# A two-block network on one core: one pair's refills in halves, two memory scores in a row, and value weights 32 bytes further

## The chip, the core and the metric

The kernel runs on one core of a Trainium2 chip. The metric is the device time of one execution in microseconds (us), the median of several. TensorE (PE) multiplies 128x128 stationary operands with streams of columns into PSUM, VectorE (DVE), ScalarE (ACT) and GpSimd (POOL) work between PSUM and SBUF, and SyncE (SP) issues the transfers from HBM. Each engine works through its own instructions in order and waits on semaphores.

## What is computed

A first block (a mixer with two convolutions, then a mixture of 32 experts, 2 of 8 in one of 4 groups for each token) and a second one of two layers (three kinds of attention, gates, attention over a memory, a feed-forward part), for 256 tokens of 1024 numbers, all in fp32. Cut to what the change touches:

```python
for e in range(N_EXPERTS):                       # first block, 32 experts
    act = jax.nn.silu(t @ w1[e]) * (t @ w3[e])
    out = out + combine[:, e:e + 1] * (act @ w2[e])

for l in range(2):                               # second block
    xn = rmsnorm_2(x, norm_mix[l])
    (qa, ka, va, qb, kb, vb, qc, kc, vc, ...) = jnp.split(xn @ w_in[l], offsets, axis=-1)
    ...
    o = rmsnorm_2(o, subln) * (1.0 - lambda_init)      # in diff_attention
    ...
    # memory_cross_attention: 4 heads of 64, 256 memory tokens
    sc = jnp.einsum('bqhd,bmhd->bhqm', q, kv[:, :, 0]) * HEAD_DIM ** -0.5
    p = jax.nn.softmax(sc, axis=-1)
    o = jnp.einsum('bhqm,bmhd->bqhd', p, kv[:, :, 1])
```

## The kernel before

**Experts.** The experts are taken in 16 pairs (PAIRS), the two of a pair side by side in 64 columns each. A pair reads w1, w3 and w2, each as two transfers of 2 MiB. They go to six slots of `ring` (w1 of even pairs to 0 and 1, w3 to 2 and 3, w2 to 4 and 5) and to two spare places in `wp` and `hs` (w1 of odd pairs). The pairs are numbered from 0; what is called the second pair here is pair 1. On PE `turn` does one pair: the w1 product and the w3 product (`expand`, L1343), the transposes of the hidden part (L1403), the way back to the tokens of the pair before (`scatter`, L1332), and the w2 product (`contract`, L1425); `gather` (L1305) brings the tokens of the next two pairs. The first two pairs stand apart from the loop over the others.

SP issues the refills in one order. `w1_done`, `w3_done` and `w2_done` tell it that a pair's product has been finished and the slots are free. For the first pair `half_done` tells it a quarter earlier each: `load_quarters` refills behind it in four parts. The w3 weights of pair 1's first expert lie elsewhere (`attic`), loaded early. From the second pair on a slot is refilled in whole transfers (`pair_after`, L815; `load`, L782). The last pair comes in halves (`last_halves`, L845).

**Layers.** The weights of a layer come in pieces of 2 MiB to `raw_a` and `raw_b`. Each piece is cut in chunks of 1024 columns a partition, and each chunk is split in a high part `w_hi` (ACT, L1748) and a low part `w_lo` (DVE, L662, some on POOL), in four buffers (PARTS) taken in turn. PE multiplies high by high, low by high and high by low. For all pieces but the values' the weights are the stationary operand and `h_parts` (or `act_parts`) the moving one, 256 columns: L1063, L1064 and L1071, and L1726 to L1729 for the last product. For the values (V_A, V_B, V_C) `h_parts` is stationary and the weights move, 512 columns: L1523 to L1525. `h_parts` is 16 floats longer than its content and read from 8 floats on (H_SHIFT), 32 bytes. In the program's layout `w_lo`, `w_hi` and `h_parts` start at multiples of 128 bytes in a partition, before and after the change alike; `moe_parts`, which holds both operands of `gather` and `scatter`, and `act_parts` start 32 bytes past one.

**Order in a layer.** The list WORK is the order by hand, and every engine takes its own part of each step. Around the memory: cross_k, cross_q 0 (queries of the first two heads, L1099 and L1104), sums, then units 24 to 27 (two heads and half of the tokens each). For a unit: scores (PE, L1579), exp (DVE scales, L2488, and reduces, L2499; ACT's exp, L1745), probs (DVE, L2505 and L2513), turn (PE transposes, L1590), apply (PE, L1611). cross_q 1 (L1063 to L1071) gives the queries of units 26 and 27; ACT copies them (L1748). cross_v (L1677) is the values of the memory.

**PSUM** is four parts of 1024 floats that the steps take in turn; a step enters one when its tenant before has left. Scores 25 take the part that the sums of the cross norm leave (DVE, L2401).

## Time and profile before

| | us |
|---|---|
| median of 3 runs | 1608.95 |
| lowest and highest | 1607.92, 1609.51 |
| the profiled execution | 1607.3 |
| its span, first to last instruction | 1605.2 |
| PE busy | 1563.0 |
| DVE busy | 880.4 |
| ACT busy | 647.6 |

The profile is of one execution. Its page gives totals and the span in 40 slices of 40.1 us; views of the trace give single instructions, the chain of work that ended last and the rates of stretches. PE's busy time counts overlapping matmuls to their modelled ends, so the distance between two starts says more than a duration. In a timeline the bracket at a row's end is the idle time before it and what ended it.

### The profile page before, as it was taken

How to read it: one execution, taken by the hardware profiler on the slowest of the kernel's cores; microseconds unless marked ns; L12 is line 12 of the kernel's file. 1: busy time of each engine (PE TensorE's matmuls, PEld its weight loads, DVE VectorE, ACT ScalarE, POOL GpSimd, SP SyncE). 2: the span in 40 equal slices, each digit the busy share in tenths (PEclk: the TensorE clock that was granted, in tenths of full speed). 3: DMA queues.
4: the chain of work that ended last, by engine and by line, in shares of the span. 5: the costliest groups of instructions: out<-in, count | busy, mean ns of one | idle time of the engine just before them, and what ended most of it. 6: DMA issues, size and time to landing. Idle time of an engine off the chain costs nothing.

```text
span 1605.2 us, 25930 instructions
## 1 busy us (share of the span) xinstructions
PE 1563.0 (97%) x11055; PEld 1261.9 (79%) x11055; DVE 880.4 (55%) x1302; ACT 647.6 (40%) x1024; POOL 58.0 (4%) x28
## 2 busy tenths in 40 slices
PE   9999999899889999999999999999999999999998
PEld 8886434334444359989899899999989999899998
DVE  6943212112121148677877676647576878576653
ACT  2034212202202135464654554435464674554443
POOL 0000000000000000033000000000006000000000
PEclk9999999999999999999999999999999999999999
DMA  9177999999999995646244456474653543465550
GB/s 351 52 314 302 383 420 427 429 428 427 430 427 428 427 403 206 197 143 200 106 158 158 151 169 206 158 266 158 197 187 121 175 158 132 127 211 180 166 210 27
DMA packets 130086, 393.86 MB, mean 245 GB/s; under 512 B 4672, under 2 KB 60352, under 8 KB 117952
## 3 DMA queue, kind: packets, MB, share of 16 engines
q1 hardware_dynamic: 129984, 392.39, 64.9%
q8 instruction: 78, 1.28, 0.3%
q14 instruction: 24, 0.20, 0.0%
HBM read 386.34 MB, written 1.05 MB: 241 GB/s over the span
## 4 chain that ended last, share of the span: by engine, by line
PE 82%; DVE 9%; DMA 7%; issue 1%; ACT 1%; SPq 0%; DVEq 0%; ACTq 0%
PE psum L1343 12%; PE psum L1063 11%; PE psum L1064 11%; PE psum L1071 11%; DMA ring<-w 6%; PE psum L1425 5%; DVE outs L2119 3%; PE psum L1728 2%; PE psum L1726 2%; PE psum L1729 2%; PE psum L1305 2%; PE psum L1579 2%; PE psum L1524 1%; PE psum L1525 1%; PE psum L1523 1%; PE psum L1023 1%
## 5 line engine op out<-in xcount | busy, mean ns | idle before, releaser
L1063 PE MATMUL psum<-h_parts,w_hi 128*128 128x256 f32 x1472 | 364.7, 286 | 1.2 <-DVE w_lo L662 1.2
L1064 PE MATMUL psum<-h_parts,w_lo 128*128 128x256 f32 x1472 | 355.1, 279 | 0.0
L662 DVE TENSOR_TENSOR w_lo<-raw_a,w_hi 128x1024 fp32r<-128x1024 f32 x186 | 225.1, 1222 | 113.1 <-ACT w_hi L1748 112.1
L1063 PEld LDWEIGHTS psum<-h_parts,w_hi 128*128 128x128 f32 x1472 | 276.1, 188 | 13.7 <-issue 10.6
L1064 PEld LDWEIGHTS psum<-h_parts,w_lo 128*128 128x128 f32 x1472 | 277.5, 189 | 0.2
L1748 ACT ACTIVATE w_hi<-raw_a 128x1024 fp32r<-128x1024 f32 x202 | 210.7, 1055 | 159.8 <-PE psum L1071 64.9
L1071 PE MATMUL psum<-h_parts,w_hi 128*128 128x256 f32 x1472 | 201.9, 279 | 0.0
L1343 PE MATMUL psum<-ring,outs 128*64 128x512 f32 x704 | 168.4, 626 | 20.5 <-DMA ring<-w 20.5
L1071 PEld LDWEIGHTS psum<-h_parts,w_hi 128*128 128x128 f32 x1472 | 184.6, 188 | 0.0
L1343 PEld LDWEIGHTS psum<-ring,outs 128*64 128x64 f32 x704 | 57.2, 144 | 124.4 <-issue 124.4
L662 DVE TENSOR_TENSOR w_lo<-raw_b,w_hi 128x1024 fp32r<-128x1024 f32 x92 | 111.4, 1221 | 53.0 <-ACT w_hi L1748 52.7
L1748 ACT ACTIVATE w_hi<-raw_b 128x1024 fp32r<-128x1024 f32 x100 | 104.8, 1055 | 87.1 <-PE psum L1071 52.9
L2321 DVE SCALAR_TENSOR_TENSOR qk<-psum,rtok,qk 128x512 f32<-128x512 f32 x16 | 18.1, 1134 | 215.7 <-PE psum L1343 215.7
L1425 PE MATMUL psum<-ring,qk 128*64 128x512 f32 x512 | 113.2, 594 | 0.0
L2314 DVE SCALAR_TENSOR_TENSOR moe_parts<-psum,rtok,moe_parts 128x512 fp32r<-128x512 f32 x34 | 24.0, 746 | 137.9 <-ACT moe_parts L1745 137.9
L1726 PE MATMUL psum<-act_parts,w_hi 128*128 128x256 f32 x328 | 91.6, 279 | 0.0
L1728 PE MATMUL psum<-act_parts,w_hi 128*128 128x256 f32 x328 | 91.6, 279 | 0.0
L1729 PE MATMUL psum<-act_parts,w_lo 128*128 128x256 f32 x328 | 91.6, 279 | 0.0
L1748 ACT ACTIVATE qk<-psum 128x512 f32<-128x512 f32 (+2 forms) x28 | 16.7, 598 | 183.6 <-PE psum L1403 160.9
L1425 PEld LDWEIGHTS psum<-ring,qk 128*64 128x64 f32 x512 | 36.9, 137 | 62.7 <-issue 62.6
L662 POOL TENSOR_TENSOR w_lo<-raw_a,w_hi 128x1024 fp32r<-128x1024 f32 x16 | 38.6, 2418 | 1175.1 <-ACT w_hi L1748 1175.1
L983 PE MATMUL psum<-hs,ring 128*128 128x256 f32 x320 | 69.5, 379 | 0.2 <-DMA ring<-w_in 0.2
(318 smaller groups left out, 2535.0 us busy)
## 6 DMA issues: line engine op xcount, KB each, us to landing
ring<-w SPq DMA_DIRECT2D x70, 2048.0 KB, 15.9
raw_a<-w_in SPq DMA_DIRECT2D x20, 2048.0 KB, 8.3
raw_a<-w_gu SPq DMA_DIRECT2D x32, 1024.0 KB, 7.7
raw_b<-w_in SPq DMA_DIRECT2D x10, 2048.0 KB, 8.9
wp<-w SPq DMA_DIRECT2D x8, 2048.0 KB, 17.9
hs<-w SPq DMA_DIRECT2D x8, 2048.0 KB, 22.2
raw_b<-w_gu SPq DMA_DIRECT2D x12, 1024.0 KB, 7.1
raw_a<-w_down SPq DMA_DIRECT2D x8, 1536.0 KB, 6.4
```

The costliest lines, as they stand in the source:

```text
L662: return eng.tensor_tensor(chunk_part(w_lo, n), chunk_raw(n), chunk_part(w_hi, n).bitcast(F32), ALU.subtract)
L983: last = mm(view(duo(name), 0, 4, SEQ)[:, o, :], w[:, k, o * P:(o + 1) * P], hT[:, k, :], start=(k == 0 and o % 2 == 0), stop=(k == KD - 1 ...
L1063: mm(to, hi[:, k, :], h_hi[:, k, :], start=(k == 0), stop=False)
L1064: mm(to, lo[:, k, :], h_hi[:, k, :], start=False, stop=False)
L1071: last = mm(to, hi[:, k, :], h_lo[:, k, :], start=False, stop=(k == KD - 1))
L1343: last = mm(psum[rows, d, bank * 512:bank * 512 + 512], duo_tokens[k // 4][:, k % 4, cols], weights, start=(k == 0), stop=(k == KD - 1), s ...
L1425: last = mm(psum[rows, 2, half * 512:half * 512 + 512], hidT[:, f, rows], view(ring[:, at + e, :], 0, 4, D)[:, f, half * 512:half * 512 + ...
L1726: mm(to, hi[:, o, :], act_hi[:, k, :], start=(k == 0 and o % 2 == 0), stop=False, skip_group_check=True)
L1728: mm(to, hi[:, o, :], act_lo[:, k, :], start=False, stop=False, skip_group_check=True)
L1729: last = mm(to, lo[:, o, :], act_hi[:, k, :], start=False, stop=(k == KF - 1), skip_group_check=True)
L1748: return nca.activation(out_ap, in_ap, ACT.Copy)
L2119: ins = v.scalar_tensor_tensor(dst[:, k, :], src[:, k, j:j + SEQ], tap, dst[:, k, :], ALU.mult, ALU.add)
```

## The change

Four edits. (1) The transfers behind the second pair (w1 of pair 3, w3 and w2 of pair 2) are issued in two halves, by the new `load_halves`: the first half waits for `half_done`, which PE now raises in the middle of each of the second pair's products too, the second half for the product's end. PE waits for the first halves by semaphores that are free by then, and pairs 2 and 3 move out of its loop to stand apart. (2) Scores 25 come before cross_q 1. (3) Each buffer of `w_lo` and `w_hi` is 8 floats longer, and a chunk starts at 0 or at 8 floats in it, so that values' chunks lie 32 bytes past a multiple of 64 and all others at one. (4) The constant `mean_sub` goes; the sums of the sub-norm use `mean_model`, and ACT's square root scales by D / (2 CH).

```diff
+HALVES_IN = 48
...
-for _name, _width in (("ident", P), ("mean_model", P), ("mean_mixb", P), ("mean_head", P), ("mean_sub", P),
+for _name, _width in (("ident", P), ("mean_model", P), ("mean_mixb", P), ("mean_head", P),
...
-           ("sums", "cross"), ("scores", 24), ("exp", 24), ("cross_q", 21, 1), ("scores", 25), ("exp", 25), ("probs", 24),
+           ("sums", "cross"), ("scores", 24), ("exp", 24), ("scores", 25), ("cross_q", 21, 1), ("exp", 25), ("probs", 24),
...
-        w_lo = sb("w_lo", [P, PARTS, KD * P], F32R)
-        w_hi = sb("w_hi", [P, PARTS, KD * P], F32R)
+        w_lo = sb("w_lo", [P, PARTS, KD * P + H_SHIFT], F32R)
+        w_hi = sb("w_hi", [P, PARTS, KD * P + H_SHIFT], F32R)
...
-            return view(parts[:, BUFFER[n], :], 0, *dims)
+            return view(parts[:, BUFFER[n], :], H_SHIFT if is_values(i) == (BUFFER[n] % 2 == 0) else 0, *dims)
...
+            def load_halves(src, q, places, k, turned, done, part_full, part_of):
+
+                sp.wait_ge(half_done, turned)
+                for e in range(2):
+                    ks = slice(0, k // 2)
+                    sp.dma_start(view(places[e], 0, k, PIECE // k)[:, ks, :], src[2 * q + e, :, ks, :]).then_inc(part_of, 16)
+                sp.wait_ge(done, 3)
+                for e in range(2):
+                    ks = slice(k // 2, k)
+                    sp.dma_start(view(places[e], 0, k, PIECE // k)[:, ks, :], src[2 * q + e, :, ks, :]).then_inc(part_full[e], 16)
...
                     load_quarters(2, w2_v, 1, 4, 4, w2_done, x_half)
+                    load_halves(w1_v, 3, spare, KD, MIX_HALVES + 10, w1_done, spare_full, win1_part[1])
+                    load_halves(w3_v, 2, ring_at[1], KD, MIX_HALVES + 11, w3_done, full_at[1], ident_in)
+                    load_halves(w2_v, 2, ring_at[2], 4, MIX_HALVES + 12, w2_done, full_at[2], consts_in)
                 else:
...
-                pair_after(0, 0)
+                    pair_after(0, 0)
...
-                    if signal and quarter < 3:
+                    if quarter in signal:
                         last.then_inc(half_done, 1)
...
-                signal, second = early_pair == 0, early_pair == 1
+                signal = {0: (0, 1, 2), 1: (1,)}.get(early_pair, ())
+                second, third, fourth = (early_pair == i for i in (1, 2, 3))
...
+                    if fourth:
+                        pe.wait_ge(win1_part[1], HALVES_IN)
...
+                    if third:
+                        pe.wait_ge(ident_in, HALVES_IN)
...
+                    if third:
+                        pe.wait_ge(consts_in, HALVES_IN)
...
-                for pair in range(2):
-                    turn(p * PAIRS + pair, p, p * (PAIRS // 2), p * (PAIRS - 1) + pair, pair, None, pair)
-                with pe.Fori(1, PAIRS // 2 - 2) as q:
+                for n in range(4):
+                    turn(p * PAIRS + n, p, p * (PAIRS // 2) + n // 2, p * (PAIRS - 1) + n, n % 2, None, n)
+                with pe.Fori(2, PAIRS // 2 - 2) as q:
...
-                                last = mm(duo("subln")[:, at:at + 2], sq[:, k, t * P:(t + 1) * P], c("mean_sub")[:, 0:2],
+                                last = mm(duo("subln")[:, at:at + 2], sq[:, k, t * P:(t + 1) * P], c("mean_model")[:, 0:2],
...
-                        f(sub_roots, duo("subln")[:, 0:16], ACT.Sqrt, bias=eps[:]).then_inc(std_ready, 1)
+                        f(sub_roots, duo("subln")[:, 0:16], ACT.Sqrt, bias=eps[:], scale=D / (2 * CH)).then_inc(std_ready, 1)
```

SP's queue behind the quarters of the first pair, before: the last quarter of w2, then the refills behind the second pair (w1 to wp and hs, w3 and w2 to the ring), then the loop.

```order
L807 DMA ring<-w2 128x1024 [waits w2_done]
L807 DMA ring<-w2 128x1024
L782 DMA wp<-w1 128x4096 [waits w1_done]
L782 DMA hs<-w1 128x4096
L782 DMA ring<-w3 128x4096 [waits w3_done]
L782 DMA ring<-w3 128x4096
L782 DMA ring<-w2 128x4096 [waits w2_done]
L782 DMA ring<-w2 128x4096
L836 UNCONDITIONAL_BRANCH
```

The same place after the change:

```order
L816 DMA wp<-w1 128x2048 [waits half_done]
L816 DMA hs<-w1 128x2048
L820 DMA wp<-w1 128x2048 [waits w1_done]
L820 DMA hs<-w1 128x2048
L816 DMA ring<-w3 128x2048 [waits half_done]
L816 DMA ring<-w3 128x2048
L820 DMA ring<-w3 128x2048 [waits w3_done]
L820 DMA ring<-w3 128x2048
L816 DMA ring<-w2 128x2048 [waits half_done]
L816 DMA ring<-w2 128x2048
L820 DMA ring<-w2 128x2048 [waits w2_done]
L820 DMA ring<-w2 128x2048
```

Six transfers of 4096 floats a partition became twelve of 2048, the first two of each four behind `half_done`.

PE at the memory scores of a layer, before: the sums of the cross norm (L1086), scores 24, cross_q 1 (16 products in turn by L1063 and L1064, then L1071), and scores 25, scores 26 and the half of 27 in one row of five; then turn 24 and cross_v 0.

```order
L1086 MATMUL psum<-consts,std 128x2 x2
L1579 MATMUL psum<-qk 128x256 x2
L1063 MATMUL psum<-h_parts,w_hi 128x256
L1064 MATMUL psum<-h_parts,w_lo 128x256
...
L1071 MATMUL psum<-h_parts,w_hi 128x256 x8
L1579 MATMUL psum<-qk 128x256 x5
L1590 MATMUL psum<-consts,wp 128x128 x4
L1677 MATMUL psum<-raw_a,memT 128x256 x8
```

After (line numbers are those of the changed file, 15 or 22 higher here):

```order
L1101 MATMUL psum<-consts,std 128x2 x2
L1601 MATMUL psum<-qk 128x256 x4
L1078 MATMUL psum<-h_parts,w_hi 128x256
L1079 MATMUL psum<-h_parts,w_lo 128x256
...
L1086 MATMUL psum<-h_parts,w_hi 128x256 x8
L1601 MATMUL psum<-qk 128x256 x3
L1612 MATMUL psum<-consts,wp 128x128 x4
L1699 MATMUL psum<-raw_a,memT 128x256 x8
```

The two products of scores 25 moved ahead of the 24 of cross_q 1; nothing else moved.

## Rows read from the trace of the kernel before

**Rows 1.** The page: engines, clock and DMA in 40 slices, costliest groups.

```profile
PE   9999999899889999999999999999999999999998
...
DMA  9177999999999995646244456474653543465550
GB/s 351 52 314 302 383 420 427 429 428 427 430 427 428 427 403 206 197 143 200 106 158 158 151 169 206 158 266 158 197 187 121 175 158 132 127 211 180 166 210 27
...
L1063 PE MATMUL psum<-h_parts,w_hi 128*128 128x256 f32 x1472 | 364.7, 286 | 1.2 <-DVE w_lo L662 1.2
...
L1726 PE MATMUL psum<-act_parts,w_hi 128*128 128x256 f32 x328 | 91.6, 279 | 0.0
```

**Rows 2.** The chain that ended last: start us, us, what.

```profile
192.12 6.92 PE psum L1425 x32
...
213.93 19.32 DMA ring<-w
233.39 8.76 PE psum L1343 x32
...
245.05 3.84 PE psum L1305 x32
...
468.34 8.80 PE psum L1343 x32
...
916.35 2.80 PE psum L1104 x24
```

**Rows 3.** Timeline of PE, the second pair and the fourth: start us, us, what.

```profile
170.89 0.59 PE L1343 MATMUL psum<-wp,outs 128*64 128x512 f32 x1
...
177.76 0.59 PE L1343 MATMUL psum<-vals,outs 128*64 128x512 f32 x1
...
233.39 8.74 PE L1343 MATMUL psum<-ring,outs 128*64 128x512 f32 x32 [3.44 <-DMA ring<-w]
```

**Rows 4.** Timeline of SP's queue (SPq) behind the second pair.

```profile
177.97 0.33 SPq L782 DMA_DIRECT2D wp<-w  x1
...
184.84 39.09 SPq L782 DMA_DIRECT2D ring<-w  x10
```

**Rows 5.** Stretches; the last three numbers are granted clock, DMA share, GB/s.

```profile
560.00:580.00 20.00, 19.92 (x110) 8.72 (x108) 4.99 (x5) 2.92 (x6) 0.00 (x0) 1.00 1.01 421
178.00:182.00 4.00, 4.00 (x20) 1.35 (x18) 0.00 (x0) 0.67 (x1) 0.00 (x0) 1.00 0.91 295
199.00:204.00 5.00, 5.00 (x26) 1.67 (x24) 1.41 (x2) 2.55 (x3) 0.00 (x0) 1.00 0.82 292
172.00:178.00 6.00, 6.00 (x30) 2.11 (x28) 1.24 (x2) 0.40 (x2) 0.00 (x0) 1.00 1.02 415
204.00:228.00 24.00, 23.92 (x128) 9.95 (x126) 5.67 (x7) 3.00 (x6) 0.00 (x0) 1.00 1.00 427
292.00:296.00 4.00, 3.86 (x10) 1.39 (x12) 0.00 (x0) 0.00 (x0) 0.00 (x0) 0.50 1.01 430
```

**Rows 6.** Timeline of the memory scores, first layer; the last row is the second's.

```profile
884.51 0.17 DVE L2401 RECIPROCAL rtok<-rtok 128x2 f32<-128x2 f32 x1 [2.94 <-ACT rtok L1745]
...
887.96 0.38 ACT L1748 ACTIVATE qk<-psum 128x256 f32<-128x256 f32 x1 [0.34 <-PE psum L1071]
...
888.60 0.75 DVE L2488 TENSOR_SCALAR wp<-psum,rtok 128x512 f32<-128x512 f32 x1 [2.12 <-PE psum L1579]
...
890.18 0.69 DVE L2513 TENSOR_TENSOR wp<-wp,stat 128x512 f32<-128x512 f32 x1
...
890.93 0.66 PE L1590 MATMUL psum<-consts,wp 128*128 128x128 f32 x4 [1.34 <-DVE wp L2513]
...
1388.85 0.66 PE L1590 MATMUL psum<-consts,wp 128*128 128x128 f32 x4 [1.34 <-DVE wp L2513]
```

**Rows 7.** Timeline of PE, a values' piece, its first and last product.

```profile
655.42 0.39 PE L1523 MATMUL psum<-w_hi,h_parts 128*128 128x512 f32 x1
...
666.39 0.40 PE L1525 MATMUL psum<-w_hi,h_parts 128*128 128x512 f32 x1
```

More of the change, by code:

```diff
@@ L1353, in expand_all, with first_weights @@
                     last = expand(places, duo_tokens, pair, d, bank, (2 * quarter, 2 * quarter + 1))
-                    if signal and quarter < 3:
+                    if quarter in signal:
                         last.then_inc(half_done, 1)
                 last.then_inc(done, 1)
-            def first_weights(duos, duo_tokens, pair, d, bank, signal=False, second_half=None):
+            def first_weights(duos, duo_tokens, pair, d, bank, signal=(), second_half=None):
                 for e in range(2):
@@ L1437, in turn @@
                             last = contract(half, [f])
-                        if signal and f < 3:
+                        if f in signal:
                             last.then_inc(half_done, 1)
```

## The prediction

> **What bounds the kernel now.** I read the page's slices first [rows 1]. From about slice 4 (140 us) to slice 14 (600 us) the DMA engines run at 9 tenths and 383 to 430 GB/s: that is the expert stage, which streams 16 pairs of experts through the ring. After it PE is busy at 9 tenths to the end while DMA idles half the time: the two layers are bound by PE. Then I read the chain that ended last through the expert stage [rows 2]. Every two pairs ((468.34 - 233.39) / 4 = 58.7 us) it passes from PE to a transfer into the ring (19.32 us in the row shown) and back; the last such piece ends where the row at 468.34 us begins, and from there to the end of the stage the chain is PE's and, for a microsecond each, DVE's: the weights are there before they are needed. So in the expert stage a microsecond counts if it is taken from the DMA engines before 468 us, and in the layers if it is taken from PE. PE's own pace hides nothing more than 3.44 us at the first of these waits (the row at 233.39 us, [rows 3]): that is the ceiling on what earlier transfers can give there.
>
> **Part 1, the second pair's slots in two parts.** Before, the six transfers of 2 MiB that follow the quarters (w1 of pair 3, w3 and w2 of pair 2) are issued when the second pair has finished each product: at 177.97 and 184.84 us [rows 4], and behind the w2 product at 192.12 + 6.92 = 199.04 us [rows 2]. Did the engines stand idle for that? In a stretch with a backlog they move 427 GB/s [rows 5]. From 178 to 182 us it is 295: (427 - 295) x 4 / 427 = 1.24 us lost. From 199 to 204 us it is 292: (427 - 292) x 5 / 427 = 1.58 us lost. At 184.84 us little can be lost, because w1 (9.8 us from 178) is still in flight. Together 2.8 us.
>
> Now the first halves go out half a product earlier. The second pair's w1 product runs from 170.89 to 177.76 us [rows 3] and its w3 product to 184.8 us [rows 4], so the first halves may start at about 174.3 and 181.2 us; w2's product runs from 192.12 to 199.04 us [rows 2], its half is over at 195.6 us. At 174.3 us the quarters still move at 415 GB/s, and do so to 178 [rows 5], so 1 MiB x 2 (4.9 us) joins a queue that isn't empty, and the second halves at 178 join it too. Backlog then: 8.4 MB from 178 us ends at 178 + 19.6 = 197.6 us at the earliest, after 195.6: the second hole closes as well. The next issue, w1 of pair 4, comes at 206 us, and w2 lasts until 197.6 + 9.8 = 207.4: at most a few tenths open there.
>
> The price: a half's pieces are smaller. Quarters move 415 GB/s, the halves at the end of the stage (560 to 580 us) 421, whole transfers 427 [rows 5]. 12.6 MB in halves cost 12.6 / 0.421 - 12.6 / 0.427 = 0.4 us. Net: 2.8 - 0.4 = **2.4 us**, with ends 1.0 (only the first hole closes, less the price) and 3.4 (the ceiling). It passes to the end: transfers that come 2.4 us earlier still meet a backlog at every later issue (the pair of transfers that PE waits for at 233.39 us was issued at 213 us and takes 9.8 us by itself, so 9 to 10 us of work stood before it), and slots come free earlier by the same. The waits that PE gets are for first halves, which land before the second ones it waits for in any case; SP waits on half_done with only the second halves behind it, whose own condition comes later. What I can't tell from before: the clock. After each of those waits PE runs some microseconds at the 1.2 GHz level (granted 0.50 from 292 to 296 us, [rows 5]), and the 32 matmuls behind the wait take 8.76 and 8.80 us where 32 of w2's product take 6.92 [rows 2]. Only the last of these (468.34 us) is on the path, and it stays; all at the lower level it would be 13.8 us, so it can move by -1.9 to +5, and I count nothing.
>
> The Trainium skill says something against this part: "SBUF — State Buffer", The DMA setup-cost knee, gives each transfer a roughly fixed 2 us that doesn't scale with bytes and asks for the largest single transfer. By it, six more transfers would cost, as an estimate, 12 us. In this trace the quarters show the fixed time hidden by the queue: it isn't paid in throughput while others are in flight.
>
> **Part 2, the order of the memory scores.** Before, cross_q 1 (24 matmuls, until 887.9 us, when ACT copies it) stands between scores 24 and scores 25 [rows 6]. DVE then scales scores 25 at 888.60, reduces them, and only then makes probs 24 (890.18), for which PE waits 1.34 us (turn 24 at 890.93; the same 1.34 in the second layer at 1388.85) [rows 6]. Now scores 25 run at about 884.85 (their PSUM part is free: DVE's L2401, which frees it, is at 884.51 [rows 6]). DVE scales and reduces them from 886.5 to 888.0, since it idles 2.12 us there; probs 24 follows, and turn 24 could start at 888.9. What is late next: the five products of scores 25, 26 and half of 27 run from 887.9 to 890.93 - 1.34 = 889.59, 0.33 us each. So cross_q 1 ends 0.65 us later, at 888.55; ACT's copy of it takes 0.38; scores 26 can't start before that, at 889.0, and with the half of 27 end at 889.97. Turn 24 starts there: 890.93 - 889.97 = **0.95 us** a layer. DVE and ACT behind it move by 0.9 to 1.1 us as well, so the next turns don't wait longer. Two layers: **1.8 us**, ends 1.0 and 2.1.
>
> **Part 3, values' weight parts 32 bytes off.** No instruction is added; 288 matmuls of 512 columns read w at another place (L1523 to L1525, 96 each), with h as the stationary operand. They follow each other every (666.39 - 655.42) / 47 = 233.4 ns [rows 7], twice the 2.80 / 24 = 116.7 ns of a product of 256 columns [rows 2]. Where do the operands lie? h_parts is read 32 bytes past a multiple of 64, w at a multiple: they differ, for values as for all others. In one place both lie 32 past: gather (L1305), all in moe_parts. There a product takes 3.84 / 32 = 120.0 ns [rows 2]: 3.3 ns more at the same size. After the change values' w lies where h does. If the same place costs 3.3 ns for each load of 128 weight columns, 288 x 3.3 = +1.0 us; if it goes with streamed columns, 6.7 ns and +1.9 us; if the row of L1305 has another reason, 0. A gain can't be excluded either, since 512 columns at 2.4 GHz are 213 ns: at most 288 x 20 = 5.8 us. I take **+1.0 us**, by the only row with both operands alike.
>
> The skill speaks of this too: "TensorE: Matmul & The Clock Gate", Step-by-step, gives PE two independent read ports, one for the moving and one for the stationary operand. By it the places don't matter and the term is 0. The row of L1305 against the others doesn't agree with that, unless its 3.3 ns come from something else.
>
> The smaller edits (mean_sub replaced by mean_model with a scale in ACT's sqrt, 64 KB less of constants) change no count and no size on the path: 0.
>
> **The sum.** -2.4 - 1.8 + 1.0 = -3.2 us. The profiled execution took 1607.3 us (span 1605.2), so it becomes 1604.1; it is 1.65 us under the median of 1608.95, so against the median **1605.7 us**.
>
> **Rivals.**
> - A, as above, 1605.7: chance 0.38.
> - B, the values' places don't matter: 1604.7. For it: one row alone speaks for a cost. 0.30.
> - C, the new place serves values better than the old one, by 1 to 5.8 us: 1599 to 1603.7. For it: 233 ns are 9% above the clock's 213. Against it: all other products, with operands placed as values' are now not, have the same 9%. 0.12.
> - D, one of the two gains doesn't come: the hole at 199 us stays, or a shorter wait at 230 us only becomes a longer or colder one at 468 us, or turn 24 finds another late partner: 1606.5 to 1608.5. 0.12.
> - E, slower, by one mechanism: with rows of 1032 floats, the parts of all other pieces move too. Buffers 1 and 2 then start 64 bytes off a multiple of 128, 0 and 3 don't; before, all four were multiples of 128. If PE's reads care about 128 bytes and not 64, half of 1472 x 3 + 328 x 3 = 5400 matmuls (each line three times, [rows 1]) change by up to 3.3 ns: 2700 x 3.3 = 8.9 us, 1614.6 us. It decides from some 1900 matmuls on. Against it: nothing in the trace has such a place, so nothing for it either. 0.08.
>
> A measurement of this kernel can tell 0.2%, 3.2 us, from no change; so A lies exactly on the line, half of it on each side. Faster: 0.19 + 0.22 + 0.12 = 0.53; slower 0.08; the same 0.39. The range that leaves out C's lower part and E: 1602.5 to 1608.5.
>
> **What the profile after would show.** The rate from 178 to 182 and from 199 to 204 us at over 400 GB/s, and the wait at 233.39 us shortened from 3.44 to about 1 us, ending at 231; the last DMA piece of the chain ending near 466. Turn 24 at its wait for DVE gone and 0.4 us for ACT's copy before scores 26. Values' matmuls every 236.7 ns (A), 233.4 (B), less (C). L1063 and L1726 unchanged at 116.7 ns, else E. I'd be wrong in part 1 if the holes close and the piece at 468 us doesn't move.

## The result, and the profile after

| | before | after |
|---|---|---|
| median of 6 runs, us | 1608.68 | 1615.0 |
| lowest and highest, us | 1607.4, 1610.74 | 1611.81, 1616.06 |
| the profiled execution's span, us | 1605.2 | 1614.0 |

The changed kernel is slower: 1.0031 times the time before, with a 95% interval of 1.0021 to 1.0042, some 5 us (3.4 to 6.8; the medians above differ by 6.3). Forecast were 1605.7 us and a range of 1602.5 to 1608.5; the time lies 6.5 us above the range, where rival E of the prediction stood (1614.6 us, chance 0.08).

Names below: "the other pieces" are all weight pieces but the values'. Their w is the stationary operand (L1078, L1079, L1086, L1748 to L1751 in the changed file; L1063, L1064, L1071, L1726 to L1729 before). "Place" is an address in a partition, modulo 128 bytes where nothing else is said, as it stands in the program's layout.

The page after, in the columns of [rows 1]; its first row is the busy time of the engines, which was PE 1563.0 before.

```profile
PE 1573.5 (97%) x11055; PEld 1276.5 (79%) x11055; DVE 880.6 (55%) x1302; ACT 647.5 (40%) x1024; POOL 57.9 (4%) x28
...
GB/s 348 50 313 272 403 428 427 428 429 428 428 429 427 428 389 197 193 157 184 109 153 157 158 186 179 168 253 161 212 174 122 169 154 132 130 209 188 152 209 27
...
L1078 PE MATMUL psum<-h_parts,w_hi 128*128 128x256 f32 x1472 | 367.8, 287 | 0.0
...
L1748 PE MATMUL psum<-act_parts,w_hi 128*128 128x256 f32 x328 | 92.2, 281 | 0.0
```

The same 11055 products keep PE busy for 10.5 us more. L1078 has 367.8 us where L1063 had 364.7, L1748 92.2 where L1726 had 91.6 [rows 1]. These lines were not rewritten: only where their weights lie changed. In the GB/s row the fifth and sixth slices stand at 403 and 428, for 383 and 420 before: the holes are gone.

The chain that ended last, after, in the columns of [rows 2]:

```profile
174.43 13.75 PE psum L1358 x64
...
216.88 17.17 DMA ring<-w
234.18 7.10 PE psum L1358 x32
...
469.26 8.80 PE psum L1358 x32
...
541.56 17.01 DMA ring<-w
558.71 7.10 PE psum L1358 x32
...
1107.32 2.86 PE psum L1119 x24
```

The second pair's products begin at 174.43 us, not at 171.07, so this execution was 3.36 us late before the change could act. From there to the row at 469.26, where the last refill that [rows 2] has too lets PE go on, it is 294.83 us. Before it was 468.34 [rows 2] less 171.07, from this row of the same view of the kernel before:

```profile
171.07 13.75 PE psum L1343 x64
```

That is 297.27 us, so 2.4 us are gained. The row at 541.56 us is a further piece on DMA that [rows 2] doesn't have; PE waited 0.34 us for it. The last row of the chain after is a group of 24 products: 2.86 us where [rows 2] has 2.80.

Stretches after, in the columns of [rows 5]: the two of the prediction, and the same two 3.4 us later, where this execution has the same work.

```profile
178.00:182.00 4.00, 4.00 (x22) 1.37 (x20) 0.00 (x0) 0.66 (x1) 0.00 (x0) 1.00 1.04 421
199.00:204.00 5.00, 5.00 (x26) 1.71 (x24) 0.83 (x2) 1.54 (x3) 0.00 (x0) 1.00 1.03 424
181.40:185.40 4.00, 4.00 (x20) 1.35 (x18) 0.00 (x0) 0.63 (x1) 0.00 (x0) 1.00 1.03 430
202.40:207.40 5.00, 5.00 (x27) 1.67 (x24) 1.41 (x2) 2.55 (x3) 0.00 (x0) 1.00 1.02 424
```

Both holes are closed, 430 and 424 GB/s for 295 and 292. Timeline of PE after, at the first wait of the expert stage, at the next one, and at the memory scores (columns as in [rows 3]):

```profile
234.18 7.09 PE L1358 MATMUL psum<-ring,outs 128*64 128x512 f32 x32 [0.85 <-DMA ring<-w]
```

```profile
263.73 0.65 PE L1358 MATMUL psum<-ring,outs 128*64 128x512 f32 x2 [1.35 <-DMA ring<-w]
```

```profile
886.23 0.50 PE L1101 MATMUL psum<-consts,std 128*128 128x2 f32 x4
...
891.58 1.10 PE L1601 MATMUL psum<-qk 64*128 64x256 f32 x6 [0.56 <-ACT qk L1770]
892.61 0.66 PE L1612 MATMUL psum<-consts,wp 128*128 128x128 f32 x4
```

The wait of 3.44 us [rows 3] is 0.85 us. A wait of 1.35 us at 263.73 is new. Turn 24 (892.61) waits for DVE no more, and 0.56 us for ACT's copy stand ahead of scores 26. So parts 1 and 2 did what was forecast in the main, and the time went elsewhere: into the products.

The down product shows it best, since nothing waits there. Timeline of PE: the second product of every chunk of weights; before, two of them four chunks apart, and after, five in a row, from buffers 0, 1, 2, 3 and 0.

```profile
1039.93 0.28 PE L1728 MATMUL psum<-act_parts,w_hi 128*128 128x256 f32 x1
...
1051.13 0.28 PE L1728 MATMUL psum<-act_parts,w_hi 128*128 128x256 f32 x1
```

```profile
1043.67 0.28 PE L1750 MATMUL psum<-act_parts,w_hi 128*128 128x256 f32 x1
...
1046.50 0.28 PE L1750 MATMUL psum<-act_parts,w_hi 128*128 128x256 f32 x1
...
1049.40 0.28 PE L1750 MATMUL psum<-act_parts,w_hi 128*128 128x256 f32 x1
...
1052.31 0.28 PE L1750 MATMUL psum<-act_parts,w_hi 128*128 128x256 f32 x1
...
1055.15 0.28 PE L1750 MATMUL psum<-act_parts,w_hi 128*128 128x256 f32 x1
```

Four chunks, 96 products, took 11.20 us before (116.7 ns each) and take 11.48 us now. A chunk of 24 takes 2.83 us in buffer 0, 2.90 and 2.91 in buffers 1 and 2 (121 ns each), 2.84 in buffer 3. Buffers 1 and 2 are those whose chunks lie at 64, buffers 0 and 3 at 0. That is rival E's pattern, but buffers 0 and 3 are slower than before too.

And the values, whose places the change was about (timeline of PE after, first and last product of the piece of [rows 7]):

```profile
657.23 0.40 PE L1545 MATMUL psum<-w_hi,h_parts 128*128 128x512 f32 x1
...
668.05 0.39 PE L1547 MATMUL psum<-w_hi,h_parts 128*128 128x512 f32 x1
```

(668.05 - 657.23) / 47 = 230.2 ns, 3.2 ns less than the 233.4 of [rows 7]: they gained, about 288 x 3 = 0.9 us.

**All products.** I added the distances from each product's start to the next one's, wherever both read `w_hi` or `w_lo` and the distance is below 300 ns: some 6,540 distances of the other pieces and 282 of values. Of the other pieces they add up to 776.0 us before and 788.7 after, of values to 65.8 and 65.0. This sum is called "the pace" below. Of the 12.7 us more, up to 1.7 come from a stretch from 599.3 to 602.7 us where the granted clock was 0.50 after the change and 1.00 before it. And not all of it is lost time: the distances of 300 ns and more between such products, where PE mostly waits for the next parts of the weights, fell from 6.8 to 4.3 us; PE's idle time of 1.08 us for `w_lo` just ahead of 609 us, for one, is gone after the change. Where PE waits for weights anyway, a slower product costs nothing.

Figures by buffer below are means of the distances inside a chunk, without those over 12% above their median: with `h_parts` moving over the chunks of the feed-forward part's first weights (44 of a layer's 151), with `act_parts` over those of the down product.

### The profile page after: what moved, and what is told of

The parts are those of the page before. It is cut to its first block, busy times and chain, and to the rows that moved or that the text cites. A ratio compares the mean times of both kernels' runs of the same rounds, so it can differ in the third digit from the quotient of the medians.

```text
span 1614.0 us, 25931 instructions
## 1 busy us (share of the span) xinstructions
PE 1573.5 (97%) x11055; PEld 1276.5 (79%) x11055; DVE 880.6 (55%) x1302; ACT 647.5 (40%) x1024; POOL 57.9 (4%) x28
## 4 chain that ended last, share of the span: by engine, by line
PE 82%; DMA 10%; DVE 5%; ACT 1%; issue 1%; SPq 0%; DVEq 0%; ACTq 0%
PE psum L1078 11%; PE psum L1358 11%; PE psum L1086 11%; PE psum L1079 11%; DMA ring<-w 10%; PE psum L1445 3%; DVE outs L2141 3%; PE psum L1750 2%; PE psum L1751 2%; PE psum L1748 2%; PE psum L1601 2%; PE psum L1320 1%; PE psum L1176 1%; PE psum L1668 1%; PE psum L1669 1%; PE psum L1672 1%
## 5 line engine op out<-in xcount | busy, mean ns | idle before, releaser
L1078 PE MATMUL psum<-h_parts,w_hi 128*128 128x256 f32 x1472 | 367.8, 287 | 0.0
L1079 PE MATMUL psum<-h_parts,w_lo 128*128 128x256 f32 x1472 | 358.4, 281 | 0.0
L1078 PEld LDWEIGHTS psum<-h_parts,w_hi 128*128 128x128 f32 x1472 | 277.0, 188 | 12.2 <-issue 9.1
L1079 PEld LDWEIGHTS psum<-h_parts,w_lo 128*128 128x128 f32 x1472 | 277.1, 188 | 0.2
L1086 PE MATMUL psum<-h_parts,w_hi 128*128 128x256 f32 x1472 | 204.5, 281 | 0.0
L1086 PEld LDWEIGHTS psum<-h_parts,w_hi 128*128 128x128 f32 x1472 | 187.6, 188 | 0.0
L1358 PE MATMUL psum<-ring,outs 128*64 128x512 f32 x704 | 164.9, 614 | 21.9 <-DMA ring<-w 21.9
L1751 PE MATMUL psum<-act_parts,w_lo 128*128 128x256 f32 x328 | 92.6, 282 | 0.0
L1748 PE MATMUL psum<-act_parts,w_hi 128*128 128x256 f32 x328 | 92.2, 281 | 0.0
## 6 DMA issues: line engine op xcount, KB each, us to landing
ring<-w SPq DMA_DIRECT2D x66, 2048.0 KB, 16.7
```

Of the source, the lines that this page charges most:

```text
L1078: mm(to, hi[:, k, :], h_hi[:, k, :], start=(k == 0), stop=False)
L1079: mm(to, lo[:, k, :], h_hi[:, k, :], start=False, stop=False)
L1086: last = mm(to, hi[:, k, :], h_lo[:, k, :], start=False, stop=(k == KD - 1))
L1358: last = mm(psum[rows, d, bank * 512:bank * 512 + 512], duo_tokens[k // 4][:, k % 4, cols], weights, start=(k == 0), stop=(k == KD - 1), s ...
L1748: mm(to, hi[:, o, :], act_hi[:, k, :], start=(k == 0 and o % 2 == 0), stop=False, skip_group_check=True)
L1751: last = mm(to, lo[:, o, :], act_hi[:, k, :], start=False, stop=(k == KF - 1), skip_group_check=True)
```

## Experiments

A ratio is to the kernel before in runs on the same chip, with its 95% interval. The kernels computed everything; only orders and places differ. `P` is 128 and `KD * P` 1024 floats. Where a diff starts from "without part 3", the kernel of the first experiment is meant. Paces are of the other pieces. The smaller edits (4) were never run by themselves: they are in every kernel below.

**1. Without part 3**, from the changed kernel.

```diff
-        w_lo = sb("w_lo", [P, PARTS, KD * P + H_SHIFT], F32R)
-        w_hi = sb("w_hi", [P, PARTS, KD * P + H_SHIFT], F32R)
+        w_lo = sb("w_lo", [P, PARTS, KD * P], F32R)
+        w_hi = sb("w_hi", [P, PARTS, KD * P], F32R)
...
-            return view(parts[:, BUFFER[n], :], H_SHIFT if is_values(i) == (BUFFER[n] % 2 == 0) else 0, *dims)
+            return view(parts[:, BUFFER[n], :], 0, *dims)
```

> The changed kernel with part 3 taken out: the buffers of w_lo and w_hi are 1024 floats long again and every chunk starts at 0 in its buffer; parts 1 and 2 and the smaller edits stay. Theory (the longer buffers cost the matmuls of all pieces 1.5 to 3 ns each, some 10 us, while the other two parts bring what was forecast): ratio to the kernel before 0.9965 to 0.998, some 3 to 5 us faster, w products back at 116 to 117 ns from start to start. Rival (the loss lies in the halves, in the extra wait at 541 us or in the first stage): still within 1 us of the changed kernel, ratio about 1.003. Rival (parts 1 and 2 bring nothing to the end): ratio 1.000.

Measured: 0.9971 (0.9961 to 0.9982), 4.7 us faster than before; 1605.24 us. PE is busy for 1561.6 us. Parts 1 and 2 bring about what was forecast for them (4.2 us), and the whole loss sits in part 3.

**2. Part 3 alone**, with the smaller edits, on the kernel before.

```diff
-        w_lo = sb("w_lo", [P, PARTS, KD * P], F32R)
-        w_hi = sb("w_hi", [P, PARTS, KD * P], F32R)
+        w_lo = sb("w_lo", [P, PARTS, KD * P + H_SHIFT], F32R)
+        w_hi = sb("w_hi", [P, PARTS, KD * P + H_SHIFT], F32R)
...
-            return view(parts[:, BUFFER[n], :], 0, *dims)
+            return view(parts[:, BUFFER[n], :], H_SHIFT if is_values(i) == (BUFFER[n] % 2 == 0) else 0, *dims)
```

> The kernel before with part 3 and the smaller edits alone (buffers of 1032 floats, values' chunks 32 bytes off; constants without mean_sub). Theory: ratio 1.005 to 1.007, 8 to 11 us slower, since the changed kernel is 6.3 us slower with gains of 3 to 4 us in it. Rival (the loss lies in the halves or in the order of the scores): ratio 0.999 to 1.001.

Measured: 1.0051 (1.0036 to 1.0067), 8.2 us slower. The pace is 787.7 us, 11.7 more than before, values' is 65.0, 0.8 less, and the distances of 300 ns and more are 5.2 us for 6.8: 11.7 - 0.8 - 1.6 = 9.3 us, in line with the time (8.2, interval 5.8 to 10.8). This shows the cause: the new places that part 3 gives the other pieces' chunks slow their products. The edit has two sides, longer rows and other starts in them; experiment 5 parts them.

**3. Part 1 alone**, from the kernel without part 3:

```diff
-           ("sums", "cross"), ("scores", 24), ("exp", 24), ("scores", 25), ("cross_q", 21, 1), ("exp", 25), ("probs", 24),
+           ("sums", "cross"), ("scores", 24), ("exp", 24), ("cross_q", 21, 1), ("scores", 25), ("exp", 25), ("probs", 24),
```

> The refills in halves alone: the changed kernel with the short buffers of the kernel before and with scores 25 behind cross_q 1 again (the smaller edits stay). Theory, by the forecast's own steps and the trace of the kernel without part 3: from the tokens' gather of the first pair to the layers 2.0 us less than before (450.1 against 452.2 us), ratio 0.9987; the kernel without part 3 is then 1.9 us faster still. Rival (the transfers' gain is lost again in the tail of the stage): ratio 1.000 and 452 us. Rival (it is part 1 that gave all of the 4.8 us): ratio 0.997.

Measured: 0.9988 (0.9976 to 1.0000), 1.9 us faster. The interval reaches from 0 to 3.9 us, so the time alone shows little. This execution happened to begin its second pair at 171.18 us, nearly where the kernel before did (171.07), so its rows can be read against [rows 3] and [rows 2] directly. The chain of this kernel, then its timeline of PE at the wait:

```profile
171.18 13.75 PE psum L1358 x64
...
466.38 8.49 PE psum L1358 x32
...
538.41 17.18 DMA ring<-w
555.73 7.10 PE psum L1358 x32
```

```profile
231.13 7.09 PE L1358 MATMUL psum<-ring,outs 128*64 128x512 f32 x32 [1.07 <-DMA ring<-w]
```

The forecast had the wait at 1 us and its end at 231 us, and the last piece at 466. A stronger sign than one kernel's time is the distance from the first gather of tokens (L1305 before) to the first product that reads `w_hi`: 451.9 us before and 452.4 with part 3 alone, 449.5 to 450.6 in the fourteen profiles of kernels with part 1. So part 1 brings 1.3 to 2.9 us, in the mean 2.1.

Against the kernel without part 3 this one lacks part 2 alone. PE's timeline from the sums of the cross norm to turn 24, here (scores in the old order) and without part 3 (the new order):

```profile
881.76 0.50 PE L1101 MATMUL psum<-consts,std 128*128 128x2 f32 x4
...
889.13 0.66 PE L1612 MATMUL psum<-consts,wp 128*128 128x128 f32 x4 [1.34 <-DVE wp L2535]
```

```profile
881.71 0.50 PE L1101 MATMUL psum<-consts,std 128*128 128x2 f32 x4
...
888.07 0.66 PE L1612 MATMUL psum<-consts,wp 128*128 128x128 f32 x4
```

7.37 and 6.36 us: 1.01 us in the first layer, forecast 0.95. In the second it is 7.36 and 6.36.

**4. Values off, the others at multiples of 128**, from the kernel without part 3 (`w_hi` as `w_lo`). Is it the place, or the length of a row?

```diff
-        w_lo = sb("w_lo", [P, PARTS, KD * P], F32R)
+        w_lo = sb("w_lo", [P, PARTS * KD * P + 64], F32R)
...
-            return view(parts[:, BUFFER[n], :], 0, *dims)
+            places = (8, 24, 40, 56) if is_values(i) else (0, 32, 32, 64)
+            return view(parts, BUFFER[n] * KD * P + places[BUFFER[n]], *dims)
```

> The changed kernel with another layout of w_lo and w_hi: the chunks of all other pieces start at a multiple of 128 bytes in every buffer, values' chunks at 32 bytes past (buffers 0 and 2) or 32 bytes before (buffers 1 and 3) such a multiple; 128 bytes lie between buffers 0 and 1 and between 2 and 3. Theory (places that are no multiple of 128 cost the other pieces, rival E of the prediction): the others back at 116.5 ns in all buffers, values at 227 to 231 ns, ratio 0.996 to 0.998, 0.5 to 1.5 us faster than without part 3. Rival (what counts is the distance to h_parts or of w_hi from w_lo, modulo more than 128 bytes, since in the changed kernel the products from buffers 0 and 3, at multiples of 128, are at 118 to 118.5 ns and not at 116.5 either): some buffers stay at 118 ns or more, ratio 0.999 to 1.002.

Measured: 0.9996 (0.9986 to 1.0006). The products from buffers 0 and 3 follow each other after 116.8 ns, those from buffers 1 and 2 after 117.5. All lie at multiples of 128; 1 and 2 lie at multiples of 256, 0 and 3, like all before, 128 past one. So modulo 128 is not the whole of it: the rival of the expectation holds, and rival E, which had 128 bytes as the period, is right in kind only. Values 231.6 ns. Against experiment 1 the ratio is 4 us worse; 0.7 ns on half of the products make some 2 us of them, and the rest isn't explained.

**5. Four places in one kernel**: rows of 1032 floats as in the change, every chunk at its row's start.

```diff
-        w_lo = sb("w_lo", [P, PARTS, KD * P], F32R)
+        w_lo = sb("w_lo", [P, PARTS * KD * P + 32], F32R)
...
-            return view(parts[:, BUFFER[n], :], 0, *dims)
+            places = (0, 8, 16, 24) if is_values(i) else (0, 8, 16, 24)
+            return view(parts, BUFFER[n] * KD * P + places[BUFFER[n]], *dims)
```

> The changed kernel with buffers of 1032 floats in which every chunk, values' or not, starts at 0: buffers 0 to 3 start at 0, 32, 64 and 96 bytes past a multiple of 128. It maps the places. Theory (distance from h_parts' place counts, which is 32): products from buffer 0 at 116.5 ns, from buffer 2 at 119 to 120, from 1 and 3 unlike those: if the same place is bad for a stationary operand, as the row of L1305 has it, 120 ns; values best (227 to 229 ns) from buffer 1. Rival (only 64-byte steps count): buffers 1 and 3 as 0 and 2. Rival (a length of a row that is no multiple of 128 bytes costs by itself): all four at 118 to 120. Time between 1.000 and 1.006.

Measured: 1.0012 (1.0002 to 1.0021). Products of h from buffers 0 to 3, high and low parts: 118.0 and 118.1; 118.5 and 119.1; 119.0 and 117.5; 115.0 and 116.1. The last are less than anything in the kernel before (116.2 and 118.0), and the next experiment follows them up. Buffer 0 was expected at 116.5. Values were best from buffer 1, as expected: 228.8 ns, from the others 231.4 to 233.0. That a bad row length costs by itself falls: buffer 3 has the same length.

**6. All w at 96**: rows of 1024 floats, the tiles themselves moved.

```diff
-        w_lo = sb("w_lo", [P, PARTS, KD * P], F32R)
-        w_hi = sb("w_hi", [P, PARTS, KD * P], F32R)
+        sb("pad_0", [P, 24])
+        w_lo = sb("w_lo", [P, PARTS * KD * P + 0], F32R)
+        sb("pad_1", [P, 32])
+        w_hi = sb("w_hi", [P, PARTS * KD * P + 0], F32R)
+        sb("pad_2", [P, 8])
         raw_b = sb("raw_b", [P, PIECE])
```

> The changed kernel with buffers of 1024 floats again, every chunk at 0 in its buffer, and w_lo and w_hi themselves moved: w_lo starts 224 bytes and w_hi 96 bytes past a multiple of 256 (both 96 past a multiple of 128); h_parts' and act_parts' places modulo 256 stay. It gives all four buffers the places of buffer 3 in the run with 0, 32, 64 and 96 bytes, where a product followed another after 114.9 (high) and 116.0 ns (low). Theory (the place of the stationary operand against the moving one sets 2 to 5 ns of each product): others at 115 to 116 ns in all four buffers, values at 231 to 232 ns, ratio 0.989 to 0.993 (some 6500 products x 1 to 1.5 ns = 6 to 10 us below the kernel without part 3, which stood at 0.997). Rival (the fast buffer had another reason, such as the unequal rows): 116.5 ns or more, ratio 0.997 or more.

Measured: 0.9867 (0.9850 to 0.9884), 1587.98 us: 21 us faster than before and, by the two ratios, 26 us faster than the change. Timeline of PE, the down product, four chunks apart, and the page's first row:

```profile
1033.16 0.28 PE L1754 MATMUL psum<-act_parts,w_hi 128*128 128x256 f32 x1
...
1044.04 0.28 PE L1754 MATMUL psum<-act_parts,w_hi 128*128 128x256 f32 x1
```

```profile
PE 1543.5 (97%) x11055; PEld 1245.4 (78%) x11055; DVE 880.5 (55%) x1302; ACT 647.3 (41%) x1024; POOL 57.9 (4%) x28
```

10.88 / 96 = 113.3 ns a product, for 116.7 before. The gain over experiment 1 is about twice what I expected (16.7 us for 6 to 10): where all four buffers are good, a product takes 113.4 ns, and the 114.9 of the single good buffer, from which the expectation started, was too careful. In the input projections it isn't so even: of some 2,190 distances there a quarter are 117 ns or more, of the 2,020 of the feed-forward part's first weights 6. Some projections have 28 or 35 such distances in both layers, others none, so something besides the place of the chunk counts there. No run says what. Repeated on another chip beside experiment 11:

> The kernel with all w at 96 once more, beside the one with others 64 apart and values alike: ratio 0.9867 as before; 1588 us. The products repeat to 0.1 ns if places set them and nothing that changes from run to run.

Measured: 0.9870 (0.9852 to 0.9887). The products of h and of act_parts took 113.4 and 113.4 ns, as in the first run: the pace goes with the layout and not with the execution or the chip.

**7. w at 224 and at 96 modulo 256**, the kernel of 6 with 128 bytes between buffers 1 and 2 (and both tiles as much longer).

```diff
-            places = (0, 0, 0, 0) if is_values(i) else (0, 0, 0, 0)
+            places = (0, 0, 32, 32) if is_values(i) else (0, 0, 32, 32)
```

> Like the run with all w at 96, but w_lo and w_hi at the same place modulo 256, 224 bytes in buffers 0 and 1 and 96 bytes in buffers 2 and 3 (128 bytes lie between buffers 1 and 2). Theory, if 128 bytes are the period: 115 ns in all four. If 256 are: one pair of buffers differs from the other by about 1 ns, as 117.6 against 116.6 in the run with values off and the others on 128. Ratio 0.990 to 0.995. Rival as before: 116.5 ns or more in all.

Measured: 0.9876 (0.9859 to 0.9892); all four buffers at 113.7 to 114.1 ns with h_parts and 113.3 to 113.5 with act_parts. For this pair of places 128 bytes make 0.5 ns at most to the other pieces. For values they do: 226.8 to 230.0 ns from buffers 0 and 1, 231.9 to 233.3 from 2 and 3.

**8. h at 64**, w as before.

```diff
-H_SHIFT = 8
+H_SHIFT = 16
```

> The changed kernel with w_lo and w_hi as in the kernel before (multiples of 128, 128 past one of 256) and h_parts read from 16 floats on instead of 8: h lies 192 bytes past a multiple of 256, which is 64 from w, as h (160) from w_hi at 96. act_parts moves to 224 bytes past one. If the distance between the operands counts: products of h at 114.9 to 116 ns, ratio near 0.993. If each operand's own place counts, and w's at 96 was the good one: h's products stay at 116.5 ns or get worse, ratio 0.997 or more.

Measured: 1.0004 (0.9995 to 1.0014). h's products 117.8 ns, and those of act_parts, which moves to 96, 119.9. The distance between the operands is 64 bytes as in experiment 6, and nothing is gained. Distance alone is not the rule.

**9. h at 0**, w as before (`H_SHIFT = 0`): both operands at the same place.

> The changed kernel with w_lo and w_hi as in the kernel before and h_parts read from 0 on: h lies at the same place as w modulo 256 (128 bytes past a multiple), as both operands of L1320 lie alike, which took 120.0 ns there. act_parts moves to 96 bytes past one. If the same place costs a product with stationary w 3 ns: h's products at 119.5 to 120 ns, some 4400 of them, 14 us, ratio 1.004 to 1.007. For values, if the same place serves a moving w: 227 to 230 ns in all buffers. If the distance doesn't count: 116.5 and 233 ns, ratio 0.997.

Measured: 1.0074 (1.0057 to 1.0091). h's products take 120.0 ns from every buffer, what [rows 2] had for L1305 (3.84 / 32). But the same place isn't the same everywhere: at 32 it was 118.5 and 119.1 in experiment 5, buffer 1. And values, timeline of PE, the same piece as above:

```profile
656.50 0.40 PE L1546 MATMUL psum<-w_hi,h_parts 128*128 128x512 f32 x1
...
667.18 0.39 PE L1548 MATMUL psum<-w_hi,h_parts 128*128 128x512 f32 x1
```

10.68 / 47 = 227.2 ns, 6 less than before. The same pair of places is the worst seen for a stationary w with h_parts and the best for a moving one.

**10. The map.** Three runs with different places in buffers 0 and 1 and in buffers 2 and 3. The edits are those of 6 to 8 with other numbers; of the first:

```diff
-H_SHIFT = 8
+H_SHIFT = 0
...
+        sb("pad_0", [P, 16])
...
+        sb("pad_1", [P, 24])
...
+        sb("pad_2", [P, 8])
...
+        sb("pad_3", [P, 24])
         with ExitStack() as feed_forward:
...
+            places = (0, 0, 8, 8) if is_values(i) else (0, 0, 8, 8)
```

> The map of places, modulo 128: h_parts at 0, act_parts at 64, w_lo and w_hi at 64 in buffers 0 and 1 and at 96 in buffers 2 and 3 (rows of 1024 floats; the rest as in the changed kernel). Known so far, stationary w: h 32 with w 0, 64, 96: 116.8, 119, 113.5 ns; h 64 with w 0: 117.6; h 0 with w 0: 120.0. Theory 1 (w's own place decides, 96 is the good one): 113 to 114 ns from buffers 2 and 3, with h and with act_parts alike, and 116 to 120 from buffers 0 and 1. Theory 2 (the distance decides, and h 64 with w 0 is a case apart): h with w at 64 113 to 114 ns, act_parts at 64 with w at 64 120 ns. Theory 3 (only the pair decides, no simple rule): anything else. Ratio 0.990 to 1.003.

Measured: 0.9960 (0.9944 to 0.9976). h 0 with w 64: 113.3 to 113.9 ns. With w 96: 117.5 (high), 118.3 (low). In the down product act_parts 64 with w 64 takes 2.86 and 2.84 us a chunk (119 ns), with w 96 2.91 and 2.90 (121 ns).

> The map of places, modulo 128: h_parts at 96, act_parts at 0, w at 0 in buffers 0 and 1 and at 32 in buffers 2 and 3. Theory 2 (distance 64 is good): h with w at 32 at 113 to 114 ns; act_parts with w at 0, the same place, 120 ns as h was. Theory 1 (w's own place): none at 113 to 114 ns, w at 0 at 116.5 to 120. Theory 3: anything else, but act_parts at 0 with w at 0 should be 120.0 ns, since h at 0 with w at 0 was. Ratio 0.995 to 1.008.

Measured: 0.9983 (0.9973 to 0.9994). h 96 with w 32: 113.5 to 114.4 ns. With w 0: 118.5 to 119.0 (high), 117.3 to 118.2 (low). act_parts 0 with w 0 takes 2.84 us a chunk, 118.3 ns, where I had expected the 120.0 of h; with w 32 it is 120.4.

> The rest of the map, modulo 128: h_parts at 64, act_parts at 96, w at 32 in buffers 0 and 1 and at 96 in buffers 2 and 3. If 64 bytes of distance are good in all but the one pair seen (h 64 with w 0: 117.6): act_parts at 96 with w at 32 at 113 to 114 ns, all else 117 to 121. If h's place at 64 is itself bad for good distances only: no pair with h under 116.

Measured in one run: 1612.48 us, the before on this chip 1609.71. h 64 with w 32: 117.9 ns, with w 96: 118.4. act_parts 96 with w 32: 2.73 and 2.72 us a chunk, 114 ns; with w 96 2.84, 118.3 ns. It is what the first half of the expectation had.

The sum of the map, a stationary w with 256 moving columns, ns from start to start (h_parts moving, means of high and low parts, 506 to 7,070 distances a cell):

| h at \ w at | 0 | 32 | 64 | 96 |
|---|---|---|---|---|
| 0 | 120.0 | not tried | 113.5 | 117.8 |
| 32 | 116.9 (117.5 at multiples of 256) | 118.7 | 118.7 | 113.5 |
| 64 | 117.8 | 117.9 | not tried | 118.4 |
| 96 | 118.4 | 113.9 | not tried | not tried |

Over all pieces, the projections too, the three good cells come out at 114.2 to 114.7, the others within 0.4 of what stands here.

**11. Both kinds at their best by the map**: h_parts and act_parts at 0, the others' w at 64, values' w at 0.

```diff
-H_SHIFT = 8
+H_SHIFT = 0
...
-        w_lo = sb("w_lo", [P, PARTS, KD * P], F32R)
+        w_lo = sb("w_lo", [P, PARTS * KD * P + 64], F32R)
...
+        sb("pad_3", [P, 8])
...
+            places = (0, 32, 32, 64) if is_values(i) else (16, 16, 48, 48)
+            return view(parts, BUFFER[n] * KD * P + places[BUFFER[n]], *dims)
```

> Best places by the map, for both kinds: h_parts and act_parts at 0 modulo 128, the other pieces' chunks at 64 in all four buffers, values' chunks at 0 (64 bytes before or behind), rows of 1024 floats with 128 bytes between buffers 1 and 2. By the map (stationary w with h at 0 and w at 64: 113.6 ns; act_parts not seen at 0 with w at 64, but at 32 with 96: 113.3; moving w with both at 0: 227.3): others 113.3 to 113.8 ns, values 227 to 228, ratio 0.986, 1 us less than with all w at 96. Rival (act_parts goes by its own place, as with w at 0 where h made 120.0 and act_parts 118.4): its products at 115 ns or more, 2 us or more lost.

Measured: 0.9885 (0.9867 to 0.9902), no better than the kernel of 6. The pair act_parts 0 with w 64, not seen before, came out at 113.4 ns, as the map said. Values reached 228.6 ns from buffers 0 and 3 only; from 1 and 2, whose place differs from h's modulo 256, it was 233.3. So what two buffers won the other two lost: values' pace is 64.6 us for the 64.8 of experiment 6, and of the 1 us hoped for next to nothing was there.

## Why the prediction was wrong, step by step

**Part 1 (-2.4 us): right.** Both holes closed; 2.4 us by the chain of the changed kernel, 466.38 - 171.18 = 295.20 against 297.27, so 2.1, by the kernel of experiment 3, 2.1 in the mean of all profiles with it, and 1.9 by its ratio. The wait, its end and the last piece came where the text had them. What it could not tell, the clock, came out well at the first wait: the 32 products behind it took 7.10 us, not 8.76 [rows 2]; the granted clock was 1.00 from 234.20 to 241.20 us, where before it had been 0.53 over the first 3.6 us behind the wait. That gave nothing to the end, though, since the stage goes by its transfers: PE came early to the next refill and waited 1.35 us there, a wait that the kernel before doesn't have. The late piece on DMA in the changed kernel's chain (541.56 us) stands in that of part 1 alone too (538.41), with waits of 0.34 and 0.52 us, and not in that of experiment 1, so the halves don't always bring it. The text, with its last wait at 468 us, had no such piece.

**Part 2 (-1.8 us): right**, 1.0 us a layer; scores 26 wait 0.56 us for ACT's copy (forecast 0.4).

**Part 3 (+1.0 us): wrong, twice.** The step that failed first is "No instruction is added; 288 matmuls of 512 columns read w at another place". The other 6,700 products changed places too, by rows of 1032 floats, and their part of the change was not in the sum; it stood in rival E, at 0.08, with "nothing in the trace has such a place, so nothing for it either". That is where the text went wrong: an unknown price on 6,700 products was weighed like a remote case, while the same unknown on 288 was given a term, and the row of L1305, 3.3 ns dearer at the same shape, was read as a fact about values alone. It was the only hint in the trace that places matter to a stationary operand. E's size was nearly right by luck: it had 2,700 products at up to 3.3 ns (8.9 us), and the pace of part 3 alone shows some 6,540 distances 1.8 ns longer (11.7 us), since buffers 0 and 3 lost as well; and E's 1614.6 us holds the +1.0 us for values, which had the wrong sign.

The second failure is the sign of values' term. The row of L1305, w stationary, was applied to values, where w moves. Experiment 9 has both in one kernel: the same place cost the stationary w 3 ns and gave values 6. Case C, that the new place serves values better, had the sign right, at a chance of 0.12; its 1 to 5.8 us are a little more than the 0.8 measured.

**The sum** with the measured sizes, from the profiles before and after: -2.0 (part 1) - 2.0 (part 2) + 12.7 (the other pieces' pace) - 2.5 (shorter waits between them) - 0.8 (values) = +5.4 us, and the ratio says +5.0.

The Trainium skill's "TensorE: Matmul & The Clock Gate", Step-by-step, has loading weights and streaming columns on two independent read ports that don't disturb each other. Read as the prediction read it, no layout would change a time, and rival B would have been the result (1604.7 us). The runs don't agree with that reading: the same products took from 113.4 to 120.0 ns by layout alone. Whether it is the two ports that disturb each other, no run shows.

**The profile's warning that was there.** 116.7 ns for 256 columns, where 2.4 GHz would give 106.7, stood in the prediction only as a remark in rival C ("have the same 9%"). Experiment 6 took 3.4 of these 10 ns away. A gap of 10 ns on 6,700 products, 67 us, was the largest open item in the kernel, against 4 us for parts 1 and 2.

**What stays open.** Why a pair of places is good. Good (113 to 114 ns) were three pairs that lie 64 bytes apart, 32/96, 0/64 and 96/32 (moving operand / w), with h_parts and with act_parts alike. But h 64 with w 0 is as far apart and isn't good; act_parts at 96 with w at 0 took 118.3 ns (2.84 us a chunk, experiment 9) or 120.0 (2.88, experiment 8, 128 bytes further), so more than 128 bytes count. A rule that gives all cells was not found. The other 7 ns above 106.7 weren't explained either, nor the longer distances in some of the projections of experiment 6.

## What to carry to other kernels

A change of a buffer's length or start moves every operand that lives in it: count all the instructions that read the tile, not those for whose sake it was moved, and give an unknown price on thousands of products a wide range, not a small chance. Where PE is the bound and its products follow each other at more than their columns need, try two or three places of the stationary operand against the moving one, since here it was worth over three times the work on waits (0.9867 against 0.9971 and 1). Rows of a length that is a multiple of 256 bytes give all buffers one place modulo 256, and then one run tells whether it is good.

## What the runs showed of the hardware

- **The pace of products depends on where the operands lie.** With everything else alike, products of 128x128 by 256 columns followed each other after 113.3 to 120.0 ns from h_parts (113.3 to 121 in the down product), to 0.1 ns the same in executions of one kernel on two chips. With w moving and 512 columns it was 226.6 to 237.5 ns, by buffer and part.
- **Single executions hold accidents as large as the effects.** Each of the three profiles below has a few microseconds at the lower level of PE's clock in the layers, where the profile before has none until its last microseconds. Stretches, columns as in [rows 5], of the kernels without part 3, with part 3 alone, and with part 1 alone:

```profile
1308.00:1314.00 6.00, 6.00 (x40) 6.00 (x41) 3.18 (x4) 2.38 (x3) 0.00 (x0) 0.72 0.00 0
```

```profile
892.00:898.00 6.00, 4.74 (x16) 4.05 (x17) 4.96 (x10) 4.47 (x12) 0.00 (x0) 0.72 0.01 3
```

```profile
1386.00:1392.00 6.00, 4.73 (x16) 4.04 (x17) 4.97 (x10) 4.46 (x11) 0.00 (x0) 0.72 0.00 1
```

A granted clock of 0.72 over 6 us costs at most 6 x 0.28 = 1.7 us. The second and the third begin at turn 24, behind its wait of 1.34 us; the kernel before has the same waits and kept its clock. The first is part of why the span of the kernel without part 3 (1603.0) is only 2.2 us below that of before while its median is 4.9 below.
- **The start varies.** The first gather of tokens, which nothing in the change touches, began between 142.31 and 146.14 us in the sixteen profiles, and at 144.77 and 143.95 in the two of one and the same kernel. The changed kernel's profile was at 145.69, that of before at 142.33. Distances between two rows of one trace are free of it.
